# Four key buffers used in turn, and bias rows moved from the projection stage on, in block 2's last attention

## The reference, cut to what matters

```python
proj = (hn @ w_in).astype(jnp.float32)
fq, fk, fv, ff, mq, mk, mv, mi, mf, mo, bq, bk, bv = jnp.split(proj, idx, axis=-1)
# fox, per head: q and k are rms-normed
s = jnp.einsum('bhqd,bhkd->bhqk', qc, k) * scale
s = s + (cqc[..., None] - cum[:, :, None, :])        # cum: running sum of log_sigmoid(f_pre)
# moba, per head: q and k are rms-normed
s_own = einsum('bhqd,bhld->bhql', qc, ko) * scale - slopes * dist_own
...
return jnp.concatenate([_from_heads(y_fox), y_ml, _from_heads(y_moba)], axis=-1)
```

## Time and profile before

| | us |
|---|---|
| time, median of 3 runs | 2509.34 |
| lowest and highest run | 2507.38, 2515.93 |
| the profiled execution's own time | 2507.15 |
| its span, first to last instruction | 2505.3 |
| projection stage of group 1, on PE | about 1865 to 1958.4 |
| attention stage of group 1, on PE | 1962.7 to 2079.6 |

### The profile page before, as it was taken

One profiled execution on the slowest core, in us unless ns is written; L12 is line 12 of the kernel. 1 busy time (PEld: TensorE's weight loads), 2 busy tenths in 40 slices (PEclk: granted clock), 3 DMA queues, 4 the chain that ended last, 5 costly groups with the idle time before them and its releaser, 6 DMA issues. The chain is left out here.

```text
span 2505.3 us, 25385 instructions
## 1 busy us (share of the span) xinstructions
PE 2070.7 (83%) x7625; PEld 1307.4 (52%) x7625; DVE 1729.9 (69%) x3556; ACT 604.7 (24%) x1397; POOL 1031.4 (41%) x1083
## 2 busy tenths in 40 slices
PE   4985766889786986777889878887969797999999
PEld 4963544545342443343544433433449664788887
DVE  4856526999987876777767788888747553545464
ACT  2124312343232221122212232322121321101121
POOL 0001013667776776776766677777720000000000
PEclk9996787999988998898999998889989877999999
DMA  4751016999999999999999999999964101233322
GB/s 172 272 200 67 18 57 243 376 396 387 409 408 403 375 404 397 406 405 404 390 403 403 404 405 387 377 407 397 409 226 134 71 1 58 77 100 85 83 84 100
DMA packets 263737, 676.48 MB, mean 270 GB/s; under 512 B 22605, under 2 KB 111042, under 8 KB 263618
## 3 DMA queue, kind: packets, MB, share of 16 engines
q0 software_dynamic: 147456, 536.94, 54.7%
q1 hardware_dynamic: 116162, 138.13, 16.5%
HBM read 672.87 MB, written 2.10 MB: 269 GB/s over the span
## 5 line engine op out<-in xcount | busy, mean ns | idle before, releaser
L2201 PE MATMUL bank<-arena 128*128 128x512 f32 x1536 | 800.5, 654 | 171.9 <-DMA arena<-in_peer_v,arena 147.5
L2432 DVE SCALAR_TENSOR_TENSOR arena<-arena,h_ps 128x1024 f32<-128x1024 f32 x512 | 614.9, 1217 | 172.8 <-DMA arena<-in_peer_u,arena 165.1
L2164 POOL DMA_INDIRECT arena<-in_peer_v,arena x512 | 504.0, 984 | 249.1 <-issue 128.6
L2164 POOL DMA_INDIRECT arena<-in_peer_u,arena x512 | 512.2, 1000 | 227.5 <-issue 131.9
L2201 PEld LDWEIGHTS bank<-arena 128*128 128x128 f32 x1536 | 295.3, 206 | 520.8 <-issue 270.9
L2445 DVE SCALAR_TENSOR_TENSOR x<-arena,x 128x1024 f32<-128x1024 f32 x128 | 164.7, 1287 | 42.8 <-DMA arena<-in_peer_v,arena 31.0
L2286 ACT ACTIVATE arena<-ident,arena 128x128 f32<-128x128 f32 x384 | 135.9, 393 | 55.2 <-PE bank L2201 34.4
L142 DVE CAST parts<-arena 128x2048 fp32r<-128x2048 f32 (+4 forms) x60 | 68.1, 1136 | 112.5 <-DMA arena<-in_w_gate_up 72.1
L1453 PE MATMUL bank<-hT,arena 128*128 128x256 f32 x512 | 122.8, 397 | 18.6 <-DMA arena<-in_peer_w_q 17.2
L144 DVE TENSOR_TENSOR parts<-arena,parts 128x2048 fp32r<-128x2048 f32 (+4 forms) x60 | 126.7, 2111 | 4.5
L1453 PEld LDWEIGHTS bank<-hT,arena 128*128 128x128 f32 x512 | 102.1, 200 | 45.7 <-DMA arena<-in_peer_w_q 18.6
(11 more groups left out here) (414 smaller groups left out, 3335.5 us busy)
## 6 DMA issues: line engine op xcount, KB each, us to landing
arena<-in_w_ada SPq DMA_DIRECT2D x12, 2048.0 KB, 9.8
arena<-in_w_in SPq DMA_DIRECT2D x15, 1536.0 KB, 6.6
arena<-in_w_gate_up SPq DMA_DIRECT2D x44, 512.0 KB, 4.9
arena<-in_peer_w_q SPq DMA_DIRECT2D x16, 1024.0 KB, 16.2
arena<-in_w_down SPq DMA_DIRECT2D x22, 512.0 KB, 3.5
arena<-in_peer_u,arena POOLq DMA_INDIRECT x512, 8.8
arena<-in_peer_v,arena POOLq DMA_INDIRECT x512, 8.5
arena<-in_w_in SPq DMA_DIRECT2D x7, 1024.0 KB, 8.8
```

The source lines that it names most:

```text
L2164: nc.gpsimd.indirect_dma_start(out=ring[:, n % R, :], out_offset=None, in_=a[table][0], in_offset=bass.IndirectOffsetOnAxis(ap=expert[:, s ...
L2201: ins = nc.tensor.matmul(psum[half][:, :], diag[:, m % R, :], v_ring[:, n % R, half * 512:(half + 1) * 512], start=(s % PH == 0 and j == 0 ...
L2432: nc.vector.scalar_tensor_tensor(out=u_ring[:, n % R, :], in0=u_ring[:, n % R, :], scalar=1.0, in1=h_ps[:, :], op0=ALU.mult, op1=ALU.mult, ...
```

## The change

- `kT_b` moves to arena column 20992 and shrinks from 12 places to 4, used in turn. That place holds the convolution's buffers until its last result is there.
- The one semaphore `row_moved` becomes four, one for each place.
- The rows of heads 0 to 3 are moved by SP at the end of its list in the projection stage, behind the last weight load, once the convolution (`conv_ready`) and the gates (`g2_done`) are done.
- The rows of heads 4 to 11 are moved by SP in the attention stage, now behind the loads of `w_out` and of the gain, each once both scores of head h-4 are done.
- Every softmax score of this attention waits for the row of its own head, instead of the first waiting for all 12. Copying k of head h waits for the scores of head h-4.
- The rms norm of q and k is placed earlier: squares of block 1 behind tile 6's copy (they stood behind tile 7's), `rms_exp` behind tile 7's (was tile 8's), the sums behind the splits 6 and 7 (were 7 and 8), the scaling behind the splits 8 and 9 (both were behind 9).

```diff
                 if p.rows_in_k:
+                    pe.wait_ge(rows_moved[h % len(p.kT)], 16 * (h // len(p.kT) + 1))
                     if h == 0:
-                        pe.wait_ge(row_moved, 16 * SM_H)
                         pe.wait_ge(ones_ready, 1)
...
-        kT_b, qT_b = view(0, SM_H, T), view(6144 + 2048, 2, GT)
+        KT_SLOTS = 4
+        rows_moved = [sem(f"row_moved{i}") for i in range(KT_SLOTS)]
+        kT_b, qT_b = view(20992, KT_SLOTS, T), view(6144 + 2048, 2, GT)
+
+        def move_row(sync, h):
+
+            if h < KT_SLOTS:
+                sync.wait_ge(conv_ready, 2)
+                sync.wait_ge(g2_done, 2)
+            else:
+                sync.wait_ge(scored, 3 * UNITS + 2 * (h - KT_SLOTS) + 2)
+            sync.dma_start(kT_b[HD:HD + 1, h % KT_SLOTS, :], gate_of[1].bias[h:h + 1, :]).then_inc(rows_moved[h % KT_SLOTS], 16)
+
         with nc.Block() as block:
             @block.sync
             def _(sync):
                 for i in range(2, S0):
                     load_b(sync, i)
+                for h in range(KT_SLOTS):
+                    move_row(sync, h)
...
                     if i == 5:
                         rms_square(act, 1, 0)
+                    if i == 6:
+                        rms_square(act, 1, 1)
                     if i == 7:
-                        rms_square(act, 1, 1)
-                    if i == 8:
                         rms_exp(act, 1)
...
-                    if i == 7:
-                        rms_reduce(dve, 1, 0)
-                    if i == 8:
-                        rms_reduce(dve, 1, 1)
-                for b in range(2):
-                    rms_scale(dve, 1, b)
+                    if i in (6, 7):
+                        rms_reduce(dve, 1, i - 6)
+                    if i in (8, 9):
+                        rms_scale(dve, 1, i - 8)
...
-                             [qT_b[:, i, :] for i in range(2)], [kT_b[:, h, :] for h in range(SM_H)],
+                             [qT_b[:, i, :] for i in range(2)], [kT_b[:, i, :] for i in range(KT_SLOTS)],
...
             def _(sync):
-                for h in range(SM_H):
-                    sync.dma_start(kT_b[HD:HD + 1, h, :], gate_of[1].bias[h:h + 1, :]).then_inc(row_moved, 16)
                 sync.dma_start(w_out_b[0][:, 0:3, :], w_out_all[:, 0:KFOX, :]).then_inc(w_out_loaded, 16)
                 sync.dma_start(w_out_b[0][:, 3:6, :], w_out_all[:, KFOX + KML:KD, :]).then_inc(w_out_loaded, 16)
                 sync.dma_start(w_out_b[1], w_out_all[:, KFOX:KFOX + KML, :]).then_inc(w_out_loaded, 16)
                 sync.dma_start(ml_gain_b, a["ml_h_g_2"].to_broadcast([P, ML_W])).then_inc(ml_gain_loaded, 16)
+                for h in range(KT_SLOTS, SM_H):
+                    move_row(sync, h)
```

## The result

| | before | after |
|---|---|---|
| median, us (9 runs each) | 2507.38 | 2493.10 |
| lowest to highest | 2500.38 to 2515.93 | 2491.35 to 2499.94 |
| profiled execution, us | 2507.15 | 2492.88 |

The ratio is 0.9945, 95% interval 0.9929 to 0.9960: 13.8 us less, between 10 and 18. The direction was right, the size was not, and neither was the range. Three more comparisons of the changed kernel with before gave ratios of 0.9957, 0.9954 and (with one empty instruction more, on a slower chip) 0.9975, which is 10.8, 11.5 and 6.5 us less. So 13.8 was the largest of four.

The account below looks back on a forecast made before the run. PE was taken to set the pace in the softmax heads, with an 8.91 us hole before them. Rows 6.1 us plus projection 1.85 us gave 8.0 us less: 2501.3 us against a median of 2509.34, range 2497 to 2506.

Parts of the forecast that it names:

- The wait for the rows: Attention's start: rows arrive early, so the first score waits only for k's copy; 6.1 us less, bounds 0 and 6.93.
- The norm in the projection: Projection: tile 9's 2.64 us wait becomes 1.3 and 1.2, its clock stays up; 1.85 us less, bounds -1.6 and +1.85.
- Added waits and later rows: Softmax heads: 22 extra score waits cost 0 (at most 1.1 us); rows 4 to 11 arrive in time, cost 0.
- The clock in the attention: Attention stage: half-clock stretches may shift with the earlier start; taken as 0, bounds -1.7 and +1.7 us.
- The rival of a clock that stays down: Softmax heads at half clock: 1.5 us more per head, 18 us for all twelve; slower, 2519 us; chance 0.05.
- the forecast sum: Whole kernel: 6.1 us from the rows plus 1.85 us from the projection, 8.0 us less; chance 0.55.
- The range: Whole kernel's time: 2497 to 2506 us around the predicted 2501.

Follow-up runs that it names:

- rows_only: The changed kernel with the norm's pieces back at their old places, so only the buffers, row moves and waits are new; ratio to before 0.9969, repeated 0.9963.
- norm_only: The kernel before with only the norm's pieces moved as in the changed kernel; ratio to before 0.9988, repeated 0.9997.
- warm: The changed kernel with 36 useless matmuls on PE behind tile 9, filling the border before the attention; ratio to before 0.9938.
- sums_late: The changed kernel with DVE's sums behind splits 7 and 8 and scalings behind split 9, as before; ACT's squares and rms_exp stay early; ratio to before 0.9954.
- its empty variants: The kernel before with one empty GpSimd instruction, in the last attention or the next stage; ratios to before 0.9988 and 1.0004 (attention), 1.0002 (next stage).
- after_again: The changed kernel, no edit, timed beside before and profiled a second time; ratio to before 0.9957.
- after_c: The changed kernel, no edit, timed and profiled a third time; ratio to before 0.9954.
- sig_late: sums_late with ACT's sigmoid and its table loads moved from the projection's end to the attention's end; median 2486.79 us, ratio to before 0.9928.
- ml_half: sig_late with one useless full-row matmul of 256 columns in each of the eight mLSTM units; median 2482.43 us, ratio to before 0.9919.
- ml_warm: sig_late with one useless full-row matmul of 512 columns in each of the eight mLSTM units; ratio to before 0.9902.
- combined2: ml_half with eight useless matmuls in the border behind tile 9, after a wait for tile 7's copy; median 2480.13 us, ratio to before 0.9895.
- after_nop: The changed kernel with one empty GpSimd instruction at the last attention's start, on a slower chip; ratio to before 0.9975.

## Why the prediction was right or wrong

1. **The wait for the rows: right.** 6.1 us forecast; the hole went from 8.9 to 2.9 us in both profiles of rows_only and in after, to 2.1 to 2.6 in the others of the changed kernel. What is late next, the copy of k, was named, and the score follows the turn by 0.88 us where I had written 0.8.
2. **The norm in the projection: right.** Forecast waits: DVE 5.5, PE 1.3 and 1.2 us, tile 9 at full clock. Measured: 5.68, 0.93, 1.26, and 1.00. The 0.93 is the idle time that the row prints. By the distance of two starts, as the forecast was made, tile 7 starts 1.1 us late: 1.27 us after the last matmul ahead of it, at 1928.81, where 0.17 is usual. Forecast sum 1.85 us; the projection took 109.2 us in the mean of seven profiles with the old order and 107.7 in seven with the new one (after's four, norm_only's two, warm), 1.5 us less. sums_late, with neither wait, shows the two from the other side.
3. **Added waits and later rows: right.** No score waited for a row. In the stretches at full clock the heads lie 4.66 to 4.67 us apart, as before.
4. **The clock in the attention: mis-sized.** This is the term that I took as 0 with bounds of 1.7 us. The runs show 53.7 us for the softmax heads at full clock and 57.5 to 63.0 in all versions of before and after, so half clock costs 4 to 9 us there. And the term isn't neutral to the change: with the new norm order the return was late in most profiles, 4.3 us worse than at 10 us. I had read "0.50 until 1979.4" off one profile, and bounded its shift by the length of one other piece. The better bound was in the same rows: half clock costs half of its length wherever PE is the limit. The rival of a clock that stays down had the price too low as well: it took tile 9's ratio of 7.4 to 5.6, but only 3.3 of these 7.4 us were at half clock. By the price above (0.48 us for each us) I estimate some 45 us more than in before for twelve heads at half clock, not 18.
5. **The sum against what is compared.** Behind the turn the changed kernel's four profiles took 645.9 us in the mean, the five of before and its empty variants 651.2: 5.3 us less, 7.6 less in the two where the clock came back within 10 us. So the forecast sum is borne out where the clock came back early, and the late return took the rest. In the two first profiles alone it was 9.5: the hole 6.05, the projection 2.6, the mLSTM heads 1.0 and the stages behind them 0.8 less, the softmax heads 1.0 more. The four comparisons of times, as differences of the means (13.5, 11.2, 8.5 and 6.2) weighted by their precision, give 10.1 us less, plus or minus 1.9 (95%).
6. **The range: the step that failed.** I set its lower end by the bounds of the changed stages and 2 us between the lowest of three runs and their median. I didn't count that the long stages ahead scatter by themselves. The turn lay from 1847.3 to 1861.8 us in the profiles on the ordinary chips, and before's own times reached from 2495.6 to 2521.2 in 35 runs. In the pair compared first, 4.7 of the 14.2 us are this scatter, in stages that no term of the sum held. The baseline moved as well: its medians were 2509.3 (3 runs), then 2507.4, 2505.1, 2507.1, 2504.5, and on two more chips 2501.4 and 2507.1. From a baseline near 2506 the same 8.0 us give 2498, inside the range. But scatter isn't all of it: the changed kernel's median was below 2497 in all three comparisons on ordinary chips (2493.1, 2494.3, 2495.9).

**What stays open.** 10.1 us in the times stand against 5.3 in the profiles. A part may be that the profiles happened on the late return more often than the timed executions did (four draws), a part that the turn came early by chance. Another part lies in a late group among before's own times: 28 of its 123 runs on ordinary chips took 2512.3 us or more, and none between 2510 and 2512. The two profiles with a turn at 1858.8 and 1861.8 were of executions of 2511.6 and 2511.8 us, 7 and 15 above the medians of their kernels. Of the changed kernel's 25 runs one lies as far out (2507.5). Without these runs, a line that I drew after seeing the times, the three differences of the means are 11.5, 9.5 and 7.5 us instead of 13.5, 11.2 and 8.5. A gain of 2 to 5 us in the unchanged stages that really belongs to the changed programs isn't excluded, and no run shows a mechanism for it. Nor do the runs say why the new norm order delays the clock's return. It goes together with the drop in tile 9: all seven profiles with that drop had the early return. That is a coincidence in time, not a cause that was shown: one and the same program (after, after_again, after_c) gave 10, 19 and 8 us. Nor does the moment of the fall sort them: in after and in sums_late the clock fell 4 us before the first score, and came back 10 and 19 us behind it.

## What to carry to other kernels

Follow a moved step through each engine's list with the old durations: here this gave 6.1 us and both new waits within 0.2 us, and it showed beforehand that the norm's new place would hold a split back twice. The same lists then gave an order without either wait (sums_late), though its 2.5 us don't stand out in the timed runs. But set the range by the scatter of the whole program, and profile the kernel before more than once: one profile can't tell which of its clock levels is the rule. And where PE idles for some us between two dense stages, look for what the other engines still do there; in sig_late's profile, moving ScalarE's 3 us out of the border gave more (3.3 us of border and, against the versions with the old border, 4 to 9 us of clock) than the norm's rearrangement. ml_half had the same short border and lost the clock all the same.

## What the runs showed of the hardware

- Half clock after a border: with 4.28 us of PE idle, the first scores ran at 0.50 in all 14 profiles that had that border and no filling. With the border filled or cut to about 1 us they ran at 1.00 in four of five (warm, sig_late, ml_warm, combined2; not ml_half).
- The mLSTM heads ran at 0.50 for 47 us though PE printed as busy for 43.5 of them. With one 128-row matmul more in each unit they took 42.8 us, all but the last 6 at full clock. Their score and decay matmuls have 64 and 4 rows, the turns and value products 128. "Busy" in the profile doesn't tell whether the clock will be granted.
- A 2 KB row moved from SBUF to SBUF landed in 1.6 to 1.7 us on an idle queue, in 3.7 to 5.1 us right behind a load of 1 MB, and in 6.0 us (7.9 in after_nop) when issued while the loads of `w_out` were under way; in after it came in 0.5 us behind the last of them.
- One chip took 2588 us for the kernel that takes 2501 to 2507 on others, with all of the difference ahead of the turn, where the rows of experts are gathered by DMA; the ratio of two kernels must come from one chip.
